# Moving a kernel's activation arena 160 bytes up in SBUF, to the same offset within 1024 bytes as its split weights

## The reference

```
for l in range(2):
    h = mod(rmsnorm(x));  x = x + 0.5*(1+g1) * (silu(h @ w1) * (h @ w3)) @ w2     # FFN 1, 2816 inner channels
    h = mod(rmsnorm(x))
    proj = h @ w_in        # RG-LRU x, gelu gate, two qkv sets, 8 forget logits, 3 merge gates
    ya = gelu(rg_gate) * rg_lru(conv(rg_x))
    yb = stick_breaking_attention(qkv_b);   yc = forgetting_attention(qkv_c)
    x = x + (1+g2) * (s0*(ya @ w_rg) + s1*(yb @ w_sb) + s2*(yc @ w_fox)) @ w_o
    h = mod(rmsnorm(x));  x = x + 0.5*(1+g3) * (silu(h @ w1') * (h @ w3')) @ w2'  # FFN 2
out = mod(rmsnorm(x))
```

## The kernel before

| | before | within 1024 | within 512 | after | within 1024 |
|---|---|---|---|---|---|
| `h_hi` | 32,896 | 128 | 128 | 32,896 | 128 |
| `h_lo` | 49,280 | 128 | 128 | 49,280 | 128 |
| `w_hi` (first of 4) | 73,856 | 128 | 128 | 73,856 | 128 |
| `w_lo` (first of 4) | 90,240 | 128 | 128 | 90,240 | 128 |
| constants (`ident_r` to `mask_fx`) | 112,832 to 115,424 | several | 192 or 224 | the same | several |
| arena's base, `g_hi`, `ya_hi`, `yf_hi` | 116,704 | 992 | 480 | 116,864 | 128 |
| `ys_hi` | 149,472 | 992 | 480 | 149,632 | 128 |
| `g_lo` | 161,760 | 992 | 480 | 161,920 | 128 |
| `mx_hi`, `q_hi` | 182,240 | 992 | 480 | 182,400 | 128 |

## Time and profile before

### The profile page before, as it was taken

How to read it: one execution, slowest core, us unless ns; L and a number is a source line. 1 busy time by engine, 2 the same in 40 slices (tenths; PEclk the granted TensorE clock), 3 DMA queues, 4 the chain that set the end, 5 groups by cost and what they waited for, 6 DMA issues and landing times.

```text
span 2766.9 us, 31911 instructions
## 1 busy us (share of the span) xinstructions
PE 2683.0 (97%) x13172; PEld 2247.2 (81%) x13172; DVE 1288.2 (47%) x1612; ACT 1060.9 (38%) x1598; POOL 1163.0 (42%) x468
## 2 busy tenths in 40 slices
PE   3999999999999999999999999999999999999998
PEld 3888888878888878888888888888788888888887
DVE  6566337875543143511056663478545422453111
ACT  5232227654344244222252232566444442523223
POOL 2555444432223434545435554354223234345442
PEclk9999999999999999999999999999999999999999
DMA  5655533221112323523245554322112122253322
GB/s 222 213 183 198 175 123 104 89 73 61 62 61 69 99 85 130 179 95 99 96 141 189 201 190 162 102 92 89 64 61 69 62 77 95 82 189 123 102 97 76
DMA packets 90833, 323.82 MB, mean 117 GB/s; under 512 B 10048, under 2 KB 12480, under 8 KB 90432
## 3 DMA queue, kind: packets, MB, share of 16 engines
q1 hardware_dynamic: 90688, 321.78, 34.1%
HBM read 319.64 MB, written 2.10 MB: 116 GB/s over the span
## 4 chain that ended last, share of the span: by engine, by line
PE 88%; DVE 6%; ACT 4%; issue 1%; POOL 1%; DMA 0%; SPq 0%; ACTq 0%; DVEq 0%
PE bank L1277 27%; PE bank L1276 27%; PE bank L1275 27%; PE bank L1310 2%; PE bank L1426 1%; PE bank L1315 1%; DVE e_lo L1101 1%; DVE e_hi L1099 1%; PE bank L1459 1%; DVE e_f L1094 1%; POOL w_lo L448 1%; DVE ada L1175 1%; DVE gt L1001 1%; ACT w_hi L478 1%; PE bank L1473 1%
## 5 line engine op out<-in xcount | busy, mean ns | idle before, releaser
L448 POOL TENSOR_TENSOR w_lo<-raw,w_hi 128x1024 fp32r<-128x1024 f32 x440 | 1142.8, 2608 | 1491.1 <-ACT w_hi L478 1490.7
L1275 PE MATMUL bank<-h_hi,w_hi 128*128 128x512 f32 x2240 | 876.5, 391 | 9.5 <-POOL w_lo L448 9.5
L1276 PE MATMUL bank<-h_lo,w_hi 128*128 128x512 f32 x2240 | 874.2, 390 | 0.0
L1277 PE MATMUL bank<-h_hi,w_lo 128*128 128x512 f32 x2240 | 874.1, 390 | 0.0
L478 ACT ACTIVATE w_hi<-raw 128x1024 fp32r<-128x1024 f32 x440 | 464.2, 1057 | 972.9 <-PE bank L1277 901.5
L1275 PEld LDWEIGHTS bank<-h_hi,w_hi 128*128 128x128 f32 x2240 | 421.8, 188 | 98.2 <-issue 10.2
L1277 PEld LDWEIGHTS bank<-h_hi,w_lo 128*128 128x128 f32 x2240 | 421.5, 188 | 88.5
L1276 PEld LDWEIGHTS bank<-h_lo,w_hi 128*128 128x128 f32 x2240 | 421.8, 188 | 87.4
L845 DVE CUSTOM_DVE_ANT_0 ada<-ada,c_act 128x1024 f32<-128x1024 f32 x144 | 284.0, 1979 | 238.6 <-DMA ada<-ada_w 238.3
L1277 PE MATMUL bank<-g_hi,w_lo 128*128 128x512 f32 (+1 forms) x792 | 295.2, 373 | 0.0
L1276 PE MATMUL bank<-g_lo,w_hi 128*128 128x512 f32 (+1 forms) x792 | 292.3, 369 | 0.0
(11 more groups left out here) (212 smaller groups left out, 3005.6 us busy)
## 6 DMA issues: line engine op xcount, KB each, us to landing
raw<-w_units SPq DMA_DIRECT2D x440, 512.0 KB, 3.5
ada<-ada_w SPq DMA_DIRECT2D x144, 512.0 KB, 4.8
ada<-ada_w SPq DMA_DIRECT2D x8, 1024.0 KB, 16.6
x<-x_in SPq DMA_DIRECT2D x4, 512.0 KB, 6.7
wab_raw<-wab SPq DMA_DIRECT2D x2, 1024.0 KB, 5.7
y<-fin SPq DMA_DIRECT2D x8, 256.0 KB, 2.1
c_act<-c_rows SPq DMA_DIRECT2D x1, 512.0 KB, 3.8
vec<-vecs SPq DMA_DIRECT2D x3, 92.5 KB, 3.6
```

The source lines that it names most:

```text
L448: nc.gpsimd.tensor_tensor(w_lo[s][:, :, :], raw[u % RAW][:, :, :], w_hi[s][:, :, :].bitcast(F32), ALU.subtract).then_inc(unit_lo.sem, 1)
L1275: nc.tensor.matmul(o, wh, xh, start=start, stop=False, skip_group_check=True)
L1276: nc.tensor.matmul(o, wh, xl, start=False, stop=False, skip_group_check=True)
L1277: return nc.tensor.matmul(o, wl, xh, start=False, stop=stop, skip_group_check=True)
```

## The change

The offset at which `w_hi` begins is noted, and the arena's base is raised to the next byte that has the same offset within 1024. That is 160 bytes further up, from 116,704 to 116,864. The arena's tensor is made 160 bytes longer so that its end moves too. No instruction is added, removed, moved or reshaped, and no transfer changes in size.

```diff
         raw = [sb(f"raw{i}", [P, UB, P]) for i in range(RAW)]
+        w_base = nc.sbuf_base
         w_hi = [sb(f"w_hi{i}", [P, UB, P], F32R) for i in range(RING)]
         w_lo = [sb(f"w_lo{i}", [P, UB, P], F32R) for i in range(RING)]
...
-        base = (nc.sbuf_base + 31) // 32 * 32
+        base = nc.sbuf_base + (w_base - nc.sbuf_base) % 1024
         ARENA = 110720
-        sb("arena", [P, ARENA // 4])
+        sb("arena", [P, (base - nc.sbuf_base + ARENA) // 4])
```

## The result

| | before | changed |
|---|---|---|
| median | 2769.89 us (2768.7 to 2770.74, 5 runs) | 2755.63 us (2749.08 to 2757.43, 5 runs) |
| ratio | | 0.9942, 95% interval 0.9927 to 0.9956 |
| span of the profiled execution | 2766.9 us | 2753.9 us (its own time 2755.63) |

What follows compares the result with a forecast made beforehand. TensorE, busy 97% of the span, was taken as the bound, so matmul pace counts. The terms, 19.4 - 1.0 + 1.0 + 0.6 = 20.0 us, put on the median 2769.68 gave 2749.7 us, range 2744 to 2765.5.

Steps and rivals of the forecast that it cites:

- a part only: Rival for the arena's 512-wide triplets: equal offsets give only 5 ns each, 4.8 us, time 2764.8 us; chance 0.08.
- What the addresses say: Operand offsets in SBUF: distances by multiples of 512 do no harm; the arena's 352 bytes off gives 0.700 us triplets.
- Term 1: 968 512-wide triplets with moving operand in the arena, weights in the rings: 20 ns saved each, 19.4 us.
- Term 2: 240 256-wide triplets from the arena (176 from g, 64 from mx): already 120 ns a step, saving nothing.
- the 256-wide steps stay near 120 ns: Sign to check in the changed kernel's time-ordered view: 256-wide matmuls keep their step.
- Term 3: Stick-breaking heads: six faster w_rg units only lengthen TensorE's wait for e_lo, so 1.0 us is not gained.
- Terms 4 and 5: Fewer slow starts at 48 stream switches, 1.0 us; products inside the arena (values), 0.6 us, suffix constants 0.
- no change: Rival: the region of the arena, not its offset, sets the step; time 2769.7 us; chance 0.13.
- The step that failed: Other engines' buffers move too but run beside TensorE; weight supply keeps up with a unit every 5.44 us.
- a new wait: Sign if g falls but the time does not: TensorE would show new waits, first of all on w_lo.
- slower by equal offsets: Rival: both operand reads hit the same place; 2774.5 us if a tenth of arena triplets, 2818 if all; chance 0.05.
- The likeliest case: Full gain from giving the arena the weights' offset, own range 2744 to 2753 us; chance 0.74.

Runs made afterwards that it cites:

- e2: Changed kernel with a 32-byte pad before x, moving every tensor up with distances kept: 2748.34 us.
- e9: Kernel before, arena at its old place, with VectorE's rounding of ya for odd channel tiles put off: 2769.14 us, 0.9998 of the kernel before.
- e12: Repeat of e7 without edit, on the same chip as e9: 2747.2 us, 0.9924 of the kernel before.
- e1: Changed kernel with a 160-byte pad between h_lo and raw, moving weights and arena up but not h: 2789.36 us.
- e3: Changed kernel with the arena 512 bytes further up: 2755.13 us.
- e4: Changed kernel with the arena 96 bytes further down: 2763.48 us.
- e5: Changed kernel with the arena 64 bytes further down: 2765.37 us.
- e6: Changed kernel with the arena 128 bytes further down: 2763.72 us.
- e11: Changed kernel with the arena 64 bytes further up: 2755.67 us.
- e7: Changed kernel with VectorE's rounding of ya for odd channel tiles put off behind the next two tiles' convolution and split: 2746.36 us, ratio 0.9916 to the kernel before.

## Why the prediction was right, and what it left out

The time fell into the range, and it moved as forecast; the forecast size of 20.0 us is what the address is worth (20.3 between the spans of before and e2, 21.9 between e9 and e12), and the changed kernel shows 14.3 of it. The address mechanism was right. That 2755.63 lies in the range is in part luck: the case with that mechanism ended at 2753, and the range went on to 2765.5 only to take in a rival, a part only, that is not what happened.

The sum can be held against the traces of before and e2, which have nearly the same half-clock steps (30 and 31) and the same waits in all (74.4 us). Every distance of starts on TensorE, less the wait if one is shown, is counted to the stream that it begins in:

| stream | gain in e2 |
|---|---|
| `g`, `ya`, `mx`, `ys`, `yf` against the rings, 512 wide | 12.4 + 2.4 + 1.9 + 1.4 + 1.3 = 19.4 us |
| of this, the steps over to the next stream | 0.6 |
| `g` and `mx`, 256 wide | 0.0 |
| `values`: 512 wide and 384 wide / 256 wide | 0.6 / -0.6 |
| `xa` | 0.4 |
| `suffix` and scores | -0.1 |
| `h`, 512 and 256 wide (clock included) | 0.7 |

- **What the addresses say.** Right in its argument, and shown by e1 and e2: in the streams against the rings only the distance counts. That multiples of 512 do no harm is shown by e3. The rule is looser than I made it, 256 suffices. One thing does not fit "only": in the 512-wide `values`, whose operands both lie in the arena and kept their distance, the triplet went from about 0.705 to 0.686 us, and to 0.699 in e1. What stands behind that is open.
- **Term 1, 19.4 us.** Right: 0.680 in `g` and `mx`, and 18.8 us inside the five streams, without the steps over to others; a few `ya` units run at half the clock, where there is nothing to gain. The down products give 3.1 us each, 12.4 in all, for 12.3. `w_o` has 45.11 us from its first matmul to `sum_squares` before and 44.15 after, 1.0 in each layer, for 96 x 0.020 = 1.9 in both.
- **Term 2, nothing.** Right: e2 and the changed kernel keep about 0.360 for three 256-wide steps. That it must be so for any distance, as "the 256-wide steps stay near 120 ns" may be read, is not so (e4, e5, e6, e11).
- **Term 3.** Right: the wait for `e_lo` grew by 1.0 us.
- **Terms 4 and 5, 1.6 us together.** About 1 us. The switches give 0.6 us out of the arena's streams and 0.4 in `xa`, for 1.0 in term 4. `values` gives nothing for 0.6: what its wide triplets gain its 256-wide ones, which the sum did not have, lose. That the whole is met within 0.3 us is more than one execution of each kernel can be trusted for.
- **The two pages of the Trainium skill,** TensorE: Matmul & The Clock Gate, section "Step-by-step: what each phase is for" (two read ports), and SBUF — State Buffer, section "SBUF: two separate sides" (TensorE waits for nobody), by which nothing would have changed, do not hold in this respect: the matmuls of `h` take 0.680 before and 0.700 in e1, at the same clock, with 160 bytes more between `h` and the weights. The 216 ns of "Back-to-back issue gap" are what that section calls the isolated gap; for a stream with weight loads it has about 131 ns, and the trace disagrees with that still more.
- **The step that failed** is the sentence that the other engines' buffers run beside TensorE, and that in its place nothing of theirs comes to the path. I had costed VectorE and GpSimd at nothing because they keep pace on average. In the RG-LRU stage VectorE's `xa_lo` came 0.3 us too late for TensorE already, and `ya_lo` ahead of it stood 80 ns in front of a GpSimd instruction that can hold it up for 2 us. In the changed kernel the order is the other way round, and with it come a stall of 4.7 us and a fall of the clock, 6.3 us in all, in the profiled execution. I named a new wait as what could go wrong, but on `w_lo`; it is on `xa_lo`.

The rivals: no change and part only fall with e1 and with the 0.680 of the changed kernel; slower by equal offsets falls too. The likeliest case had the right mechanism, and its own range of 2744 to 2753 holds e2, e7 and e12 but not the changed kernel's median.

## What to carry to other kernels

Read steps from the distance of starts, in two streams that differ in one thing alone: here that one comparison, 0.700 against 0.680, gave 19.4 us of a change worth about 20. On a TensorE-bound kernel, look at the distance of the moving operand's start from the weights' start, try a multiple of 256 bytes first (here 0, 256 and 512 gave the shortest 512-wide steps) and a few others, and expect other widths to want another. Before gains are added up, look where another engine's result arrives only just in time and which of its instructions stand within some tens of ns of an instruction that can hold it up, here VectorE's subtractions beside GpSimd's. Work that nobody waits for can be moved out of that chain; it took 9 us off the changed kernel and nothing off the one before.

## What the runs showed that I had not expected

- For 512-wide fp32r matmuls with 128 x 128 weights the step is 226.7 ns at a distance of 0 or 256 bytes within 512, 229 ns at 64, and 233 to 234 ns at 352, 384, 416 and 448. For 256-wide ones from `g` it is 113 ns at 448, 117 at 416, 118 at 64, 119 at 384, and 120 at 0, 256 and 352.
- Two instructions that start 10 to 100 ns apart on VectorE and GpSimd decide over 2.2 us of VectorE's time, and by way of the granted clock over 6 us of the whole. In e2 `ya_lo` was first by ten nanoseconds and there was no stall; in the changed kernel it was second by twenty.
- The best version found is the changed kernel with the late `ya` split: 2746.4 us, 0.9916 of the kernel before, with the ten executions of e7 and e12 within 4.2 us of each other, where the changed kernel's cover 15.
